# First expert tiles with one 512-wide product per step, their low half summed by VectorE between its routing steps, and 100 candidate sums per head in place of 256

## What is computed

```python
q = (xc @ wq).reshape(C, PEER_HEADS, 2, half)
s = jnp.einsum('thpd,hpkd->thpk', q, subkeys)
sv, si = lax.top_k(s, PEER_TOPK)                       # 16 of 128, on 2 sides, 8 heads
cand = (sv[:, :, 0, :, None] + sv[:, :, 1, None, :])   # 16 x 16 sums per head
fs, fi = lax.top_k(cand, PEER_TOPK)                    # the best 16 of them
g = jax.nn.softmax(fs, axis=-1)
a = jax.nn.gelu(jnp.einsum('tc,thkc->thk', xc, u_tab[eid]))
out = jnp.einsum('thk,thkc->tc', g * a, v_tab[eid])
```

## Time and profile before

| | |
|---|---|
| median of 3 runs | 2036.26 us (2035.74 to 2036.82) |
| profiled execution | 2035.02 us, of it the span 2033.2 us |
| PE, PEld busy | 100%, 89% |
| DVE, ACT, POOL busy | 63%, 53%, 79% |
| granted PE clock | 1.00 |
| HBM read | 356.49 MB, 176 GB/s |

### The profile page before, as it was taken

One profiled execution on the slowest core, in us unless ns is written; L12 is line 12 of the kernel. 1 busy time (PEld: TensorE's weight loads), 2 busy tenths in 40 slices (PEclk: granted clock), 3 DMA queues, 4 the chain that ended last, 5 costly groups with the idle time before them and its releaser, 6 DMA issues.

```text
span 2033.2 us, 43867 instructions
## 1 busy us (share of the span) xinstructions
PE 2024.1 (100%) x13396; PEld 1803.2 (89%) x13396; DVE 1280.6 (63%) x2665; ACT 1081.0 (53%) x2325; POOL 1602.6 (79%) x1316
## 2 busy tenths in 40 slices
PE   9999999999999999999999999999999999999999
PEld 8989899998888888888889898999988888888887
DVE  6786599688888333333367765996888873333333
ACT  6564655544444555555565556445444455555554
POOL 7777978887777888888877678888877778888886
PEclk9999999999999999999999999999999999999999
DMA  9544645544444555555584445455444445555554
GB/s 268 175 142 138 208 158 179 185 168 152 145 154 150 190 189 194 196 190 192 196 235 156 135 149 203 164 179 184 166 153 146 149 150 196 192 191 194 194 190 153
DMA packets 103391, 358.37 MB, mean 176 GB/s; under 512 B 11744, under 2 KB 16802, under 8 KB 103076
## 3 DMA queue, kind: packets, MB, share of 16 engines
q1 hardware_dynamic: 102900, 355.41, 53.2%
q10 hardware_dynamic: 432, 2.18, 0.3%
HBM read 356.49 MB, written 1.05 MB: 176 GB/s over the span
## 4 chain that ended last, share of the span: by engine, by line
PE 82%; POOL 9%; issue 8%; DVE 0%; ACT 0%; DMA 0%; POOLq 0%; SPq 0%; DVEq 0%; ACTq 0%
PE bank L1861 34%; PE bank L1508 15%; POOL w_lo L429 9%; PE bank L1510 8%; PE bank L1481 6%; PE bank L1485 6%; PE bank L1483 6%; PE bank L1801 4%; PE bank L1780 1%; DMA xT<-x_in 0%; DVE raw_lo L916 0%; ACT raw_hi L541 0%; POOLq L427 0%; POOLq L450 0%; ACT w_hi L492 0%
## 5 line engine op out<-in xcount | busy, mean ns | idle before, releaser
L429 POOL TENSOR_TENSOR w_lo<-ring,w_hi 128x512 fp32r<-128x512 f32 x1048 | 1401.4, 1353 | 340.1 <-ACT w_hi L492 339.6
L492 ACT ACTIVATE w_hi<-ring 128x512 fp32r<-128x512 f32 x1312 | 753.9, 621 | 368.9 <-PE bank L1485 317.1
L429 DVE TENSOR_TENSOR w_lo<-ring,w_hi 128x512 fp32r<-128x512 f32 x256 | 236.6, 924 | 450.1 <-ACT w_hi L492 449.9
L1481 PE MATMUL bank<-act_parts,w_hi 128*128 128x256 f32 x1536 | 440.5, 287 | 0.9 <-POOL w_lo L429 0.8
L1483 PE MATMUL bank<-act_parts,w_hi 128*128 128x256 f32 x1536 | 434.5, 283 | 0.0
L1485 PE MATMUL bank<-act_parts,w_lo 128*128 128x256 f32 x1536 | 434.5, 283 | 0.0
L1861 PE MATMUL bank<-w_hi,e_hi 128*128 128x512 f32 x1024 | 398.9, 390 | 0.2
L1861 PE MATMUL bank<-w_hi,e_lo 128*128 128x512 f32 x1024 | 398.4, 389 | 0.0
L1861 PE MATMUL bank<-w_lo,e_hi 128*128 128x512 f32 x1024 | 398.4, 389 | 0.0
L1508 PE MATMUL bank<-act_parts,w_hi 128*128 128x512 f32 x1088 | 385.9, 398 | 0.0
L1481 PEld LDWEIGHTS bank<-act_parts,w_hi 128*128 128x128 f32 x1536 | 294.5, 192 | 10.4 <-issue 8.0
(11 more groups left out here) (235 smaller groups left out, 2423.0 us busy)
## 6 DMA issues: line engine op xcount, KB each, us to landing
ring<-stream SPq DMA_DIRECT2D x654, 512.0 KB, 3.3
arena<-rpb_in SPq DMA_DIRECT2D x8, 512.0 KB, 8.9
arena<-dft_in SPq DMA_DIRECT2D x4, 512.0 KB, 6.3
arena<-subkeys ACTq DMA_DIRECT2D x2, 1024.0 KB, 5.7
xT<-x_in SPq DMA_DIRECT2D x4, 256.0 KB, 5.7
ring<-stream SPq DMA_DIRECT2D x4, 256.0 KB, 5.9
arena<-w_in SPq DMA_DIRECT2D x2, 512.0 KB
arena<-decay_in SPq DMA_DIRECT2D x2, 512.0 KB
```

The source lines that it names most:

```text
L429: eng.tensor_tensor(w_lo[:, part_, :], ring[:, tile % RING, half * HT:(half + 1) * HT], w_hi[:, part_, :].bitcast(F32), ALU.subtract).then ...
L492: nc.scalar.activation(w_hi[:, 2 * (tile % AHEAD) + half, :], ring[:, tile % RING, half * HT:(half + 1) * HT], ACT.Copy).then_inc(hi_ready ...
L1481: T.matmul(out_, weights(w_hi, tile, j), hi[:, k, :], start=start, stop=False, skip_group_check=True)
```

## The change

The first 60 expert tiles of each layer go through `wide_tile`. ScalarE copies the low half of tile n into `first_lo` (four slots, at the place of expert rows 80 to 83), before it splits tile n + 2, and issues the GELU two tiles later than before. VectorE adds the low half (`sum_first`), which the GELU waits for. These sums stand between its routing steps: `worked` counts units for each step and puts one sum into the program for each 233 (`PACE`). Both halves of the routing are written out in place of a loop, `s_cur` and `best_s` and their copies are gone, and the sorted lists give 3 x 16 + 13 x 4 candidates per head (of the first three ranks all 16 partners, of the others four), from whose place the two ranks are worked out in nine short operations. The memset is cut into pieces of eight rows, the four rows of `first_lo` follow at the end, and the working copies for `slotT` lie in PSUM.

```diff
+FULL, SHORT = 3, 4
+CANDS = FULL * TOPK + (TOPK - FULL) * SHORT
+ONES = 8
+LOW_AT = 80
+PACE = 233
...
-        s_cur = part(80, 2 * PH, NK)
+        first_lo = part(LOW_AT, RING, S)
...
-        cand = part(96, PH, TOPK, TOPK)
-        cand_rest = part(104, PH, TOPK * TOPK)
+        cand = part(96, PH, CANDS)
...
+                def first_low(i, n):
+
+                    act.wait_ge(tile_done.sem, tile_done.at(l, i * RING + (T_U + n + 1)))
+                    nc.scalar.activation(first_lo[:, n % RING, :], bank[n % 4][:, S:2 * S], ACT.Copy
+                                         ).then_inc(first_lo_ready.sem, 1)
+
                 def gelu(i, n):
+
+                    act.wait_ge(first_sum.sem, first_sum.at(l, i * RING + (n + 1)))
                     nc.scalar.activation(experts[:, bass.ds(i * RING + n, 1), :].rearrange("p a t -> p (a t)"),
...
+                            first_low(i, first + s)
                             high_parts(l, i, T_U + first + s + AHEAD)
-                            gelu(i, first + s)
+                            gelu(i, first + s - 2)
...
+                for n in range(RING):
+                    first_low(0, n)
                     high_parts(l, 0, T_U + n + AHEAD)
-                    gelu(0, n)
+                    if n >= 2:
+                        gelu(0, n - 2)
+                gelus(RING, SORTED - 3 * RING)
+                for n in range(SORTED - 2 * RING, SORTED):
+                    first_low(0, n)
+                    high_parts(l, 0, T_U + n + AHEAD)
+                    if n == SORTED - RING:
+                        act.wait_ge(best_ready.sem, best_ready.at(l, 1))
+                        nc.scalar.activation(expd[:, :, :], expd[:, :, :], ACT.Exp).then_inc(expd_ready.sem, 1)
+                    else:
+                        gelu(0, n - 2)
+                    if n == SORTED - RING - 1:
+                        gelu(0, n - 1)
+                        load_table(ACT.Exp)
                 gelus(SORTED, ROUTED - SORTED)
+                gelu(0, ROUTED - 2)
+                gelu(0, ROUTED - 1)
...
+                summed = [0]
+                pending = [-400]
+
+                def sum_first():
+
+                    n = summed[0]
+                    summed[0] += 1
+                    dve.wait_ge(first_lo_ready.sem, first_lo_ready.at(l, n + 1))
+                    u_ps = bank[n % 4][:, 0:S]
+                    V.tensor_tensor(u_ps, u_ps, first_lo[:, n % RING, :], ALU.add).then_inc(first_sum.sem, 1)
+
+                def worked(units, at_most):
+
+                    pending[0] += units
+                    while pending[0] >= PACE:
+                        pending[0] -= PACE
+                        if summed[0] < at_most:
+                            sum_first()
+
+                before_exp = SORTED - RING
+                for tt in range(TT):
+                    dve.wait_ge(score_copied.sem, score_copied.at(l, 4 * tt + 4))
                     for m in range(2 * PH):
-                        step(V.max(top_s[:, m, 0:8], s_cur[:, m, :]))
-                        V.max_index(top_i[:, m, 0:8], top_s[:, m, 0:8], s_cur[:, m, :])
-                        step(V.match_replace(s_rest[:, m, :], top_s[:, m, 0:8], s_cur[:, m, :], LOWEST))
-                        step(V.max(top_s[:, m, 8:16], s_rest[:, m, :]))
+                        row = s_all[:, tt, m * NK:(m + 1) * NK]
+                        link(V.max(top_s[:, m, 0:8], row))
+                        V.max_index(top_i[:, m, 0:8], top_s[:, m, 0:8], row)
+                        link(V.match_replace(s_rest[:, m, :], top_s[:, m, 0:8], row, LOWEST))
+                        link(V.max(top_s[:, m, 8:16], s_rest[:, m, :]))
                         V.max_index(top_i[:, m, 8:16], top_s[:, m, 8:16], s_rest[:, m, :])
+                        worked(158, before_exp)
...
-                    step(V.tensor_tensor(cand[:, :, :, :], sides[:, :, 0, :].unsqueeze(3).to_broadcast(wide),
-                                         second_ps.unsqueeze(2).to_broadcast(wide), ALU.add))
+                    if tt == 0:
+                        dve.wait_ge(score_copied.sem, score_copied.at(l, 8))
+                        V.tensor_copy(keys_ps, iota_t[:, :, :].rearrange("p k t -> p (k t)").bitcast(F32))
+                        V.tensor_copy(iota_ps, iota_k[:, :])
+                    link(V.tensor_copy(second_ps, sides[:, :, 1, :]))
+                    for a0, a1, n, at in ((0, FULL, TOPK, 0), (FULL, TOPK, SHORT, FULL * TOPK)):
+                        grid = [P, PH, a1 - a0, n]
+                        link(V.tensor_tensor(cand[:, :, at:at + (a1 - a0) * n].rearrange("p h (a b) -> p h a b", b=n),
+                                             sides[:, :, 0, a0:a1].unsqueeze(3).to_broadcast(grid),
+                                             second_ps[:, :, 0:n].unsqueeze(2).to_broadcast(grid), ALU.add))
+                    worked(150, before_exp)
...
+                    V.tensor_copy(place_f[:, :], flat_i)
+                    link(V.tensor_copy(rank_f[:, :, :], rank[:, :, :]))
+                    first_of, second_of = rank_f[:, 0, :], rank_f[:, 1, :]
+                    short_at = float(FULL * TOPK - FULL * SHORT)
+                    link(V.scalar_tensor_tensor(first_of, second_of, -short_at / SHORT, first_of, ALU.add, ALU.max))
+                    link(V.tensor_scalar(second_of_ps, first_of, -float(SHORT), -short_at, ALU.mult, ALU.add))
+                    link(V.scalar_tensor_tensor(second_of_ps, first_of, -float(TOPK), second_of_ps,
+                                                ALU.mult, ALU.max))
+                    link(V.tensor_tensor(second_of, second_of_ps, place_f[:, :], ALU.add))
+                    link(V.tensor_copy(index_ps.rearrange("p h s k -> p (h s) k"), top_i[:, :, :]))
+                    worked(450, before_exp)
...
+                while summed[0] < before_exp - 1:
+                    sum_first()
...
-                link(V.memset(experts[:, ROUTED:NK, :], 1.0))
+                worked(200, SORTED)
+
+                def ones(j0, j1):
+                    link(V.memset(experts[:, j0:j1, :], 1.0))
+                    worked(22 * (j1 - j0), SORTED)
+
+                for j0 in range(ROUTED, LOW_AT, ONES):
+                    ones(j0, min(j0 + ONES, LOW_AT))
+                for j0 in range(LOW_AT + RING, NK, ONES):
+                    ones(j0, min(j0 + ONES, NK))
 
                 for tt in range(TT):
                     dve.wait_ge(slotT_done.sem, slotT_done.at(l, tt + 1))
                     cols_ = slice(tt * P, (tt + 1) * P)
                     src = bank[6 + tt][:, 0:3 * P].rearrange("p (c t) -> p c t", c=3)
+                    rest = bank[6 + tt][:, 3 * P:4 * P]
                     link(V.tensor_copy(slotT[:, 0:3, cols_], src))
-                    link(V.tensor_tensor(w_rest[:, :], src[:, 2, :], slotT[:, 2, cols_], ALU.subtract))
-                    link(V.tensor_copy(slotT[:, 3, cols_], w_rest[:, :]))
-                    link(V.tensor_tensor(w_rest[:, :], w_rest[:, :], slotT[:, 3, cols_], ALU.subtract))
-                    ins = V.tensor_copy(slotT[:, 4, cols_], w_rest[:, :])
-                    if tt == 0:
-                        link(ins)
-                link(ins)
+                    link(V.tensor_tensor(rest, src[:, 2, :], slotT[:, 2, cols_], ALU.subtract))
+                    link(V.tensor_copy(slotT[:, 3, cols_], rest))
+                    link(V.tensor_tensor(rest, rest, slotT[:, 3, cols_], ALU.subtract))
+                    ins = V.tensor_copy(slotT[:, 4, cols_], rest)
+                    link(ins)
+                    worked(220, ROUTED)
...
+                worked(80, ROUTED)
...
                 one_hots(0, 0)
+                worked(170, ROUTED)
                 one_hots(0, 1)
+                while summed[0] < ROUTED:
+                    sum_first()
+                dve.wait_ge(first_sum.sem, first_sum.at(l, ROUTED))
+                link(V.memset(experts[:, LOW_AT:LOW_AT + RING, :], 1.0))
                 dve.wait_ge(gelu_done.sem, gelu_done.at(l, ROUTED))
                 add_parts(0, 0)
...
-                    contract(bank[s % 4][:, 0:S], i, T_U + first + s).then_inc(tile_done.sem, 1)
+                    wide_tile(bank[s % 4], i, T_U + first + s, both_acts)
...
-                    pe.wait_ge(gelu_done.sem, gelu_done.at(l, i * RING + (ROUTED + n - 1)))
+                    pe.wait_ge(gelu_done.sem, gelu_done.at(l, i * RING + (ROUTED + n - (3 if n < AHEAD else 1))))
```

More of the change, by code:

```diff
@@ L215, in encoder_kernel @@
         second_ps = bank[5][:, 0:PH * TOPK].rearrange("p (h k) -> p h k", k=TOPK)
+        second_of_ps = bank[5][:, P:2 * P]
         weight_ps = bank[5][:, 0:3 * P]
@@ L1313, in dve_layer @@
+                    worked(150, before_exp)
                     for h in range(PH):
-                        c = cand[:, h, :, :].rearrange("p a b -> p (a b)")
-                        b0, b1 = best_s[:, h * TOPK:h * TOPK + 8], best_s[:, h * TOPK + 8:h * TOPK + 16]
```

(18 more changed lines are left out.)

41 lines of the change are left out of this document (9 added, 32 removed).

## The result

The changed kernel takes 2044.7 us (median of 7 runs, 2041.76 to 2048.88), the kernel before 2035.53 (7 runs, 2033.72 to 2036.82): ratio 1.0045 [1.0033, 1.0057]. It is **slower by 9 us**, outside the predicted range. The profiled execution of after is the fastest of the seven: 2041.76 us, a span of 2039.9, against 2035.02 and 2033.2. So there are two things to explain: 6.7 us between the two profiled executions, and some 2.5 us by which the medians lie further apart than these.

What follows compares the result with a forecast made beforehand. PE, busy in 100% of the span, was taken to set the time. Per layer 6.6 us gained against PE waits of 0.5 + 2.0 + 4.7 = 7.2 gave +1.1 in two layers: median 2037.4 us, range 2030 to 2042.

Steps and rivals of the forecast that it cites:

- rival 4: PE's 4.7 us wait at tile 56 lowers its clock: up to 2.77 a tile, 2040 to 2046 us; chance 0.12.
- pitch of a first tile: PE's time per first-expert tile falls from 2.88 to 2.77 us, as in the query stage.
- VectorE keeps up while it routes: Routing and 47 sums take VectorE 128 us against PE's 130, so PE does not wait there.
- exponential to sum 47: On VectorE, softmax work and the first memset piece precede the sum of tile 47: 4.8 us after the exponential.
- sum 47 to sum 52: On VectorE, memset pieces, sums and the first `slotT` block delay tile 52's sum by 19.3 us; PE waits 4.7.
- VectorE needs 401.63 to 403.75 = 2.1: VectorE's work between the exponential and the first memset takes 2.1 us, as in the trace before.
- rival 3: VectorE falls behind while routing, its two-input SBUF operations contending with POOL: 2043 to 2046 us; chance 0.12.
- The memset's price: On VectorE, 2048 memset elements cost 2.21 us with link, counting idle time ahead of the row.
- Rival 2: Faster: memsets cost only their row's time, late tiles start at 429.3, 2030.5 us, or 2023 without waits; chance 0.22.
- The sum: Per layer 6.6 us gained, 7.2 given back; two layers +1.1: profiled execution 2036.1, median 2037.4 us.
- 0.05 more moves the exponential: Sign of being wrong: a first-expert pitch 0.05 over 2.77 delays the exponential, 5 us in two layers.
- the prize: Gain from fewer PE instructions in first-expert tiles: 60 tiles x 0.11 x 2 layers = 13.2 us.

Runs made afterwards that it cites:

- e4: The changed kernel with small filler products on PE, 13 ahead of tile 51 and 23 ahead of tile 56, results unused: 2045.95 us.
- e5: e2 with 13 small filler products on PE ahead of tile 51, its only hole: 2032.95 us.
- e2: The changed kernel with memset rows counted as 27 units in place of 22 and the memset carrying sums up to tile 59: 2034.29 us.
- e9: The changed kernel with the softmax sums and reciprocals in PSUM, so each product has one SBUF and one PSUM input: 2043.47 us.
- e3: The changed kernel with only the sums of tiles 47 and 48 placed before the wait for the exponential: 2046.52 us.
- e7: e1 with all 256 candidates per head in place of 100: 2044.57 us.
- e1: The changed kernel with sums 47 and 48 before the exponential's wait, memset rows counted as 27 units and sums up to tile 59 in the memset: 2027.45 us.
- e10: e1 with two 512-column products and then two 256-column ones in wide tiles, in place of one and one: 2025.07 us.

## Why the prediction was wrong

The order of events was right, two waits behind the memset's pieces. The result lies above the range because rival 4 was real (the clock, put at nothing in the sum), because two more terms of the sum were too small (the softmax products, the chain of pieces and sums), and, by what other traces suggest, because the pitch has a second value. By the prediction's own steps, first layer:

| step | forecast | after | |
|---|---|---|---|
| pitch of a first tile | 2.77 | 2.77 (2.83 in stretches of other kernels) | half right |
| VectorE keeps up while it routes | yes | yes, sums wait at the copies | right |
| start of the exponential | 396.6 | 396.18 | right |
| exponential to sum 47 | 4.8 | 5.95 | 1.15 short |
| tile 51 starts | 402.3 | 403.11 | 0.8 |
| sum 47 to sum 52 | 19.3 | 19.80 | 0.5 short |
| tile 56 starts | 421.65 | 423.00 | 1.35 |
| from there to the late tiles | 11.1 | 12.76 | 1.7 short |
| late tiles start | 432.7 | 435.76 | 3.1 |

- **"The 4.7 us hole costs PE its clock"** was a rival with 0.12 and should have been part of the forecast. The holes were 2.83 and 3.33 long, shorter than the 4.7 on which I put that rival, and the clock fell behind both. Tile 51 took 4.44 us (403.11 to 407.55) and tile 56 took 4.33 (423.00 to 427.33), 1.6 over the pitch; the rival's "up to 2.77" bounds it. The fall behind the first hole costs nothing in the end: PE would have stood longer at tile 56, and this is why that hole is 3.33 and not 4.7. The one behind the last hole is paid in full. e4 and e5 show the clock as the cause: with PE at work in the same gap there is no fall. e4 takes both falls away and its crossing is 1.2 to 1.4 shorter, the price of the last one; e5 takes the only one away that e2 has, and tile 51 is 1.3 to 1.6 shorter. My reason against it, that the page shows no such thing before, was no reason: the longest wait of PE in the profile of before is 1.1 us.
- **"VectorE needs 401.63 to 403.75 = 2.1"** took the 1.38 us of the product pair as its price. It was the price of one product beside POOL and one in POOL's pause (1.17 and 0.28). In after both stand beside POOL: 2.47, which is 1.09 of the 1.15 us that the step is short. The prediction named the contention, for rival 3, and never moved it to this place. e9 confirms the cause, with 1.97 us off each of the two sums.
- **The memset's price** was nearly right: 2.26 per piece, where the sum has 2.21. Rival 2, which took the row's price, didn't come. The chain from sum 47 to sum 52 is 0.5 us longer than worked out: 0.3 for six pieces of 2048 at 0.05 more, most of the rest for five sums at 0.39 in place of 0.36. The `slotT` block took 1.91, as forecast.
- **The sum.** The profiled execution was to be 2036.1 and was 2041.76. The 5.7 between them are close to two layers of 3.1 from the table.
- **"0.05 more moves the exponential"** was written as a sign of being wrong, and it is what most likely parts the median from the profile. I took 2.77 from one pair of rows of one execution. After's profiled run happened to be all 2.77 in the first-expert stages; e3, e4 and e9, whose crossings cost about as much as after's, were profiled at 2046.52, 2045.95 and 2045.25 with long stretches of 2.83. That the runs of after above 2042 had them too is argued from this, since only one was traced.
- **Rival 3** (VectorE behind in routing) did not happen: the conversions of the ranks took up to 1.35 and 1.41 (the second 0.29 in before), 1.1 more each, which the 4 us of slack cover. e7 shows what the reserve was: with 256 candidates it is gone.

What of the prize was there: e1 keeps 7.5 us of the 13.2, e10 keeps 8.4 us (2033.48 before in its batch).

## What to carry to other kernels

A wait that is put on an engine's critical stream costs its length and what the engine does at half speed behind it. Here a hole of about 3 us cost 1.3 to 1.6 more, and the last one of a stage can't hide that; so sum up the holes first, and put the work that releases them ahead of anything long (two sums ahead of a wait and 27 for 22 in one count were worth 17 us). A duration that was measured beside another engine's pause holds only beside that pause: look at the minimum and the maximum of a row's instances before using its mean. And where the prize is 0.11 of a pitch of 2.88, one trace is no measurement of a pitch that can differ by 0.055 from one stretch to the next.

## What the runs showed of the hardware

- Alternating 512- and 256-column products ran at two rates, 0.346 and 0.354 us per step, for whole stretches of a stage, with the granted clock at 1.00 in both and no wait. In pairs it was 0.348, in fours 0.351, and always that in the traces taken.
- Behind a hole of 0.86 us PE kept its clock; behind 2.83 and 3.33 it went on at 2.4 GHz for a step or three and then fell to 1.2; behind 4.21 (e7), 4.66 (e9) and 7.03 (e3) it was at 1.2 from the first product on, and in e9 the granted clock is 0.50 already from 421 to 422 us, inside the hole (it ends at 422.58).
- A 128 x 128 product of two SBUF tensors on VectorE took 0.28 us without GpSimd beside it and 1.17 to 1.37 with it; with one input in PSUM it took 0.28 beside GpSimd's work (e9).
- The row of a memset of 2048 elements per partition says 1.76 us, and the next piece started 2.26 after its start (414.77 to 417.03).
